# A second way to the v rows: tiles 1 to 5 gather u alone, and their v sums come from a product with the whole v table

## The chip, the cores and the metric

One core of one Trainium2 chip. The metric is the device time of the kernel in microseconds (us), the median of the runs. The engines are TensorE (PE), VectorE (DVE), ScalarE (ACT), GpSimd (POOL) and SyncE (SP, which issues most plain transfers).

## The reference, cut to what matters

A layer of a streaming encoder: a retention and short convolution block, then PEER, a retrieval of single-neuron experts per token, then a final norm. 1024 prompt tokens and 32 sample tokens, width 1024, all in float32. The part that the change touches:

```python
        s1 = jnp.einsum('thd,hnd->thn', q[:, :, 0], keys1)
        s2 = jnp.einsum('thd,hnd->thn', q[:, :, 1], keys2)
        v1, i1 = lax.top_k(s1, PEER_TOPK)
        v2, i2 = lax.top_k(s2, PEER_TOPK)
...
        eidx = jnp.take_along_axis(cidx, sel, axis=-1)
        gate = jax.nn.softmax(top_s.astype(jnp.float32), axis=-1).astype(xb.dtype)
        act = jax.nn.gelu(jnp.einsum('td,thkd->thk', xb, u_tab[eidx]))
        return jnp.einsum('thk,thkd->td', gate * act, v_tab[eidx])
```

Every token picks 8 heads x 16 = 128 of 16384 = 128 x 128 experts. With each it takes the dot product of its vector with a row of u, and adds a row of v, weighted by gate times gelu of the dot.

## The kernel before, in words

Tokens are worked in 8 tiles of 128 and a last tile of 32. A tile has 128 **steps**, one for each expert of a token: step g gathers one row of 8 KB for each of 128 tokens (u and v stand side by side in the table `uv`), 1.05 MB in one indirect DMA that POOL issues (L985). The rows land in a ring of 7 slots, 9 from step 616 on. Then, per step: DVE takes the dot product of the u half with the tile's vectors (L2050, a custom instruction and a read of its accumulator), ACT takes the gelu (L1225), multiplies by the gate (L1241) and scales the v half of the row by it (L1245), and PE adds the scaled half into PSUM by eight transposing products with the identity (L1625). The last of these frees the slot (`slot_free`), for which POOL waits before it gathers into it again. The last tile has 32 steps whose 128 rows belong to four experts of each of 32 tokens, summed by four products of 256 columns (L1571).

The rest of the layer is spread over these steps. Every engine runs one program in order; generators yield the step at which their next piece is put, and `advance` puts all that are due. So the projections (L1311, L1344), the retention of each tile, the product with w_out (L1406), the queries (L1508) and the scores of later tiles are computed on PE while earlier tiles are in their steps. DVE chooses the experts of one head of one tile at a time (`choices`: maxima and indices of 128 and 256 scores, L1852 to L1864, then L1965 to L1982), 71 such pieces in all; 41 of them stand in steps 128 to 767, 6 in steps 768 to 825 and 10 behind. L1786 adds a table to retention products, L1722 is one tap of the convolution. Weights come by SP through three buffers (`stream`).

At the end of a tile (`finish`) ACT copies the sum out of PSUM (L1193), PE turns it back (L1565), ACT and DVE norm it, and SP stores it.

```python
                for c in range(KC):
                    ins = pe.matmul(expert_sum[:, c * P:(c + 1) * P], row_of(g)[:, D + c * P:D + (c + 1) * P],
                                    ident_sb[:, :], is_transpose=True, start=False, stop=(g + 1 == end_of(t)),
                                    skip_group_check=True)
                ins.then_inc(slot_free, 1)
```

Of the kernel before, what the change touches and what calls it, by code (L numbers as in the profile page):

```python
# [59 lines left out]
QUADS_IN = 0  # L60
SPLIT = 2


RINGS = [(0, RING), (88 * RING, RING + 2)]


def slot_of(g):

    first, slots = [r for r in RINGS if r[0] <= g][-1]
    return (g - first) % slots  # L70
# [4 lines left out]

def lap_of(g):

    return SLOTS[:g].count(SLOTS[g])


def same_slot_before(g):

    return max((b for b in range(max(0, g - 2 * RING), g) if SLOTS[b] == SLOTS[g]), default=None)
# [71 lines left out]
def sums_before_x1(t):  # L155

    return t - 2


# [5 lines left out]
def sums_before_out(t):  # L165

    return sum(end_of(u) < out_at(t) for u in range(TILES + 1))
# [264 lines left out]
def layer_kernel(nc, xT, x, w_ret, w_conv, w_out, wq, keysT, uv, g_mix, g_ffn, g_fin, conv_par,  # L432
                 ret_state, cos_sin, decay_p, decay_s, edge_p, edge_s, block_decay, ident, sel, iota,
                 y, out_ret_p, out_ret_s, out_conv_p, out_conv_s):
    with ExitStack() as ctx:
# [33 lines left out]
        dots = sb("dots", [P, RINGS[-1][1]])  # L469
        weights = sb("weights", [P, RINGS[-1][1]])  # L470
# [40 lines left out]
        squares_last = last[:, 1792:1792 + QW]  # L511

# [99 lines left out]

        def first_out_bank(i):
            return [x1_ps[:, 0:D // 2], x1_ps[:, D // 2:3 * D // 4], mm[:, 1, 0:D // 4]][i]
# [68 lines left out]
        landed = [sem(f"landed{i}") for i in range(RINGS[-1][1])]  # L683
# [4 lines left out]
        y_out = [sem("y_out0"), sem("y_out1"), sem("y_out2")]  # L688
# [30 lines left out]
        def y_stored(eng, t):  # L719
            eng.wait_ge(y_out[t % 3], 16 * (t // 3 + (QUADS if t == SAMPLE else 1)))  # L720

        def store_quarter(eng, q):
            eng.dma_start(y[SEQ:TOK, q * QW:(q + 1) * QW],
                          y_last[q * DEC:(q + 1) * DEC, :]).then_inc(y_out[SAMPLE % 3], 16)
# [8 lines left out]
        def _(sp):  # L733
# [17 lines left out]
            def load_x_ahead(t):  # L751
                n, j = rows_of(t), group_of(t)
                yield mix_at(1) + 20 if t == 4 else first_use_at(j) - (26 if t < 5 else 64)
                if residual_stays(t):
                    if t == 2:
                        sp.wait_ge(projected, use_at(0, "ret", RING, 1) + 1)
                    wait(sp, sum_started, sums_before_x1(t))
                    if t == 3:
                        sp.wait_ge(projected, use_at(0, "B", 2, 1) + 1)
# [7 lines left out]
                if t == SAMPLE:  # L767
                    sp.wait_ge(sum_started, 3)
# [111 lines left out]
            def load_x(t):  # L880
# [7 lines left out]
                elif t in (4, 7):  # L888
                    yield end_of(t - 4) + 2
                    sp.wait_ge(sum_started, sums_before_x1(t))  # L890
# [24 lines left out]

            def store_y(t):
                n = rows_of(t)
                yield sum_root_at(t) + 5
                sp.wait_ge(y_ready, t + 1)
# [4 lines left out]
                sp.dma_start(y[t * P:t * P + n, :], xn[0:n, t % 2, :]).then_inc(y_out[t % 3], 16)  # L924

            def store_states():
# [13 lines left out]
                               *[load_cs(t) for t in range(TILES + 1)], *[store_y(t) for t in range(TILES + 1)], store_states())  # L940
# [4 lines left out]
            for t in range(TILES - 2, TILES + 1):  # L945
                y_stored(sp, t)


        @block.gpsimd
        def _(pool):  # L950
            for g in range(TOTAL):
# [10 lines left out]
                if same_slot_before(g) is not None:  # L962
                    pool.wait_ge(slot_free, same_slot_before(g) + 1)
                elif g >= RING:
                    pool.wait_ge(wout_done, SAMPLE + 3)
                else:
                    pool.wait_ge(projected, use_at(0, "ret", g, 1) + 1)
# [22 lines left out]
        def _(act):  # L990
# [21 lines left out]
            def projection(j):  # L1012
                for q, (kind, unit, t, slot) in enumerate(USES[j]):
# [17 lines left out]
                    if unit in (0, 4):  # L1031
                        wait(act, x1_ready, GROUPS[j][0])
                        if t == SAMPLE and unit:
                            act.wait_ge(sum_started, 4)
# [140 lines left out]
            def finish(t):  # L1175
                n = rows_of(t)
                yield end_of(t)
                if t == SAMPLE:
# [3 lines left out]
                    act.wait_ge(slot_free, end_of(t))  # L1182
# [5 lines left out]
                    act.wait_ge(y_ready, t + 1)  # L1188
# [3 lines left out]
                act.wait_ge(slot_free, end_of(t))  # L1192
# [3 lines left out]
                act.wait_ge(sum_back, t + 1)  # L1196
# [3 lines left out]
                act.wait_ge(sum_squared, 2 * t + 1)  # L1200
# [3 lines left out]
            programs = started(*[finish(t) for t in range(TILES + 1)],  # L1204
# [11 lines left out]
            for g in range(TOTAL):  # L1216
                t, k = tile_of(g)
                d = dots[:, SLOTS[g]:SLOTS[g] + 1]
# [7 lines left out]
                if t == SAMPLE:  # L1226
                    act.wait_ge(gelu_done, g + 1)
                    act.wait_ge(weighed, g + 1)
                    if k >= 3:
                        act.wait_ge(slot_free, g - 2)  # L1230
# [8 lines left out]
                act.wait_ge(gelu_done, g + 1)  # L1239
# [903 lines left out]
```

## Time and profile before

| what | value |
|---|---|
| runs of the kernel before, median | 2945.24 us (2944.16 to 2946.45, 3 runs) |
| span of the profiled execution | 2941.5 us |
| that execution's own time | the profile has none beside its span |
| busy: PE, DVE, ACT, POOL | 2311.9, 2077.7, 1968.4, 1258.5 us |
| moved | 1205.73 MB, mean 410 GB/s |
| gathers (queue q0) | 1107.36 MB, 91.2% of 16 engines' span |

Busy times are of instructions with their overlaps taken out; the mean of one instruction is longer than its share of the busy time where they are pipelined, as on PE. PEld is the loading of PE's stationary operand, which overlaps the products. PEclk is the granted clock of TensorE as a share of 2.4 GHz, the DMA share the busy share of the 16 DMA engines. An ordinary float32 product of PE stands in the trace as two records, a transposing one as one. The program's `x1_ps` is called `x_ps` in the profile.

### The profile page before, as it was taken

To read this page: it belongs to the slowest core of one execution; us is meant where nothing else is said; L and a number is where in the kernel's file an instruction comes from. 1 tells how busy PE (TensorE), PEld (TensorE's weight loads), DVE (VectorE), ACT (ScalarE), POOL (GpSimd) and SP (SyncE) were. 2 spreads that over 40 slices of the span, in tenths; PEclk is the share of its full clock that TensorE was granted. 3 is DMA by queue.
4 is the path that set the end of the run, shared out by engine and by line. 5 is a ranking of instruction groups with operands and counts; after the bars stand their busy time and mean duration, and the time that the engine had idled before them with its cause. 6 is when DMAs were issued, how large, how long until landed. Compare 5 with 4: busy or idle time off the path is not lost.

```text
span 2941.5 us, 36244 instructions
## 1 busy us (share of the span) xinstructions
PE 2311.9 (79%) x12548; PEld 1815.8 (62%) x12548; DVE 2077.7 (71%) x5143; ACT 1968.4 (67%) x3670; POOL 1258.5 (43%) x1063
## 2 busy tenths in 40 slices
PE   9988988987787777888987888778766666666777
PEld 8877777665565556665665555555655555555556
DVE  3677788675687887777666555788868787766444
ACT  2477666677676777666667676777767666767663
POOL 0233434444343444344444445334444445555653
PEclk9999999999987879999996988988767656666669
DMA  8899999999999999999999999999999999999998
GB/s 340 323 408 404 419 416 407 414 418 421 420 409 415 416 416 411 421 420 409 419 415 410 419 421 420 420 420 420 418 421 421 418 418 413 412 419 410 421 413 338
DMA packets 182055, 1205.73 MB, mean 410 GB/s; under 512 B 21744, under 2 KB 27184, under 8 KB 43504
## 3 DMA queue, kind: packets, MB, share of 16 engines
q0 software_dynamic: 152368, 1107.36, 91.2%
q1 hardware_dynamic: 29264, 95.93, 8.4%
q8 instruction: 99, 1.62, 0.2%
q14 instruction: 84, 0.69, 0.1%
q10 hardware_dynamic: 240, 0.13, 0.0%
HBM read 1198.48 MB, written 4.86 MB: 409 GB/s over the span
## 4 chain that ended last, share of the span: by engine, by line
DMA 42%; PE 22%; DVE 21%; ACT 10%; issue 4%; POOL 1%; SPq 0%; DVEq 0%; ACTq 0%; POOLq 0%
DMA ring<-in_uv,idx 38%; PE expert_sum L1625 9%; DVE ring L2050 9%; ACT ring L1245 4%; DMA w_out_sb<-in_uv,idx 4%; PE x_ps L1406 2%; PE mm L1508 2%; PE mm L1311 1%; ACT weights L1241 1%; PE x_ps L1344 1%; PE mm L1344 1%; DVE pairs_left L1855 1%; ACT L1225 1%; PE x_ps L1311 1%; PE expert_sum L1311 1%
## 5 line engine op out<-in xcount | busy, mean ns | idle before, releaser
L985 POOL DMA_INDIRECT ring<-in_uv,idx x958 | 1137.1, 1187 | 1534.0 <-PE expert_sum L1625 1328.1
L1625 PE MATMUL expert_sum<-ident_sb,ring 128*128 128x128 f32 x7472 | 1222.4, 319 | 516.6 <-ACT ring L1245 513.7
L2050 DVE CUSTOM_DVE_ANT_0 ring<-ring,xn 128x1024 f32<-128x1024 f32 x959 | 1168.1, 1222 | 616.9 <-DMA ring<-in_uv,idx 610.8
L1625 PEld LDWEIGHTS expert_sum<-ident_sb,ring 128*128 128x128 f32 x7472 | 1022.3, 165 | 782.5 <-ACT ring L1245 711.7
L1245 ACT ACTIVATE ring<-ring,weights 128x1024 f32<-128x1024 f32 x934 | 1073.0, 1149 | 30.4
L1225 ACT ACTIVATE dots<-dots 128x1 f32<-128x1 f32 x1056 | 211.4, 200 | 789.8 <-DVE dots L2050 786.9
L1241 ACT ACTIVATE weights<-dots,gate 128x1 f32<-128x1 f32 x1024 | 301.5, 294 | 38.3 <-DVE gate L1994 1.5
L1508 PE MATMUL mm<-xn_in,stream 128*128 128x416 f32 (+1 forms) x500 | 202.9, 531 | 0.0
L1625 PE MATMUL expert_sum<-ident_sb,w_out_sb 128*128 128x128 f32 x720 | 139.2, 358 | 70.0 <-ACT w_out_sb L1245 69.8
L1625 PEld LDWEIGHTS expert_sum<-ident_sb,w_out_sb 128*128 128x128 f32 x720 | 113.6, 186 | 98.7 <-ACT w_out_sb L1245 96.3
L985 POOL DMA_INDIRECT w_out_sb<-in_uv,idx x96 | 115.8, 1206 | 124.9 <-PE expert_sum L1625 110.4
L2050 DVE CUSTOM_DVE_ANT_0 w_out_sb<-w_out_sb,xn 128x1024 f32<-128x1024 f32 x97 | 118.5, 1223 | 68.3 <-DMA w_out_sb<-in_uv,idx 67.7
L1311 PE MATMUL mm<-stream,xn_in 128*128 128x256 f32 (+1 forms) x640 | 166.4, 395 | 0.0
L1311 PEld LDWEIGHTS mm<-stream,xn_in 128*128 128x128 f32 (+1 forms) x640 | 106.8, 182 | 22.4 <-issue 4.2
L1508 PEld LDWEIGHTS mm<-xn_in,stream 128*128 128x128 f32 x500 | 91.4, 204 | 40.9 <-issue 27.1
L1245 ACT ACTIVATE w_out_sb<-w_out_sb,weights 128x1024 f32<-128x1024 f32 x90 | 103.4, 1149 | 2.9
L2050 DVE DVE_READ_ACCUMULATOR2_ANT dots<- 128x1 f32 x1056 | 86.8, 82 | 0.0
L1344 PE MATMUL mm<-xn_in,stream 128*128 128x384 f32 (+1 forms) x232 | 84.3, 496 | 2.6 <-ACT conv_tmp L1028 2.3
L1225 ACT ACT_TABLE_LOAD x50 | 64.2, 1283 | 0.9
L1311 PE MATMUL x_ps<-stream,xn_in 128*128 128x256 f32 x256 | 64.0, 383 | 0.0
L1344 PE MATMUL x_ps<-xn_in,stream 128*128 128x128 f32 (+1 forms) x240 | 60.8, 400 | 0.0
L1571 PE MATMUL mm<-ring,stream 128*128 128x256 f32 x200 | 50.0, 399 | 9.3 <-ACT stream L1231 9.3
(405 smaller groups left out, 2218.3 us busy)
## 6 DMA issues: line engine op xcount, KB each, us to landing
stream<-in_wq SPq DMA_DIRECT2D x21, 1024.0 KB, 11.7
stream<-in_w_conv SPq DMA_DIRECT2D x16, 1024.0 KB, 11.3
stream<-in_w_ret SPq DMA_DIRECT2D x16, 1024.0 KB, 9.5
ring<-in_uv,idx POOLq DMA_INDIRECT x958, 13.9
ring<-in_w_ret SPq DMA_DIRECT2D x6, 1024.0 KB, 12.5
x<-in_x SPq DMA_DIRECT2D x8, 512.0 KB, 8.3
out_y<-xn SPq DMA_DIRECT2D x8, 512.0 KB, 8.2
stream<-in_w_out SPq DMA_DIRECT2D x3, 1024.0 KB, 9.7
```

The source lines that it names most:

```text
L985: pool.indirect_dma_start(row_of(g), None, uv, bass.IndirectOffsetOnAxis(ap=rows, axis=0)).then_inc(landed[SLOTS[g]], 16)
L1225: act.activation(d, d, ACT.Gelu_apprx_tanh).then_inc(gelu_done, 1)
L1241: act.activation(w, d, ACT.Copy, scale=gate[:, t % 5, k:k + 1]).then_inc(weighed, 1)
L1245: act.activation(v, v, ACT.Copy, scale=w).then_inc(scaled, 1)
L1311: ins = pe.matmul(bank[0:n, 0:UNIT], xnj[:, k, at:at + n], weight[k], start=(k == 0), stop=(k == KC - 1))
L1344: ins = pe.matmul(bank[:, 0:columns.stop - columns.start], weight[k], moving, start=(k == 0), stop=(k == KC - 1))
L1406: ins = pe.matmul(x1_ps[0:n, i * 512:(i + 1) * 512], lhsT, w_out_of(j, k)[:, i * 512:(i + 1) * 512], start=(k == 0), stop=(k == KC - 1))
L1508: ins = pe.matmul(query_bank(m, s), weight[s][k], xnT_of_pass(m)[:, k, :], start=(k == 0), stop=(k == KC - 1))
L1571: ins = pe.matmul(last_bank, of[0:rows, 96 - q * DEC:96 - q * DEC + P], values[0:rows, q * QW:(q + 1) * QW], start=begins and q == 0, stop ...
L1625: ins = pe.matmul(expert_sum[:, c * P:(c + 1) * P], row_of(g)[:, D + c * P:D + (c + 1) * P], ident_sb[:, :], is_transpose=True, start=Fals ...
L1855: ins = dve.match_replace(rest, values[:, 0:8], s, LOWEST)
L2050: dve.tensor_tensor_reduce(u, u, xn[:, t % 2, :], 1.0, 0.0, ALU.mult, ALU.add, dots[:, SLOTS[g]:SLOTS[g] + 1]).then_inc(dotted, 1)
```

## The change

Tiles 1 to 5 (`DENSE`) gather their u rows alone: half rows of 4 KB, into 8 halves of ring slots 0 to 3. Their 640 steps consist of the gather and the dot on DVE; no scaling on ACT and no expert sum on PE. The dots of a whole tile are kept (`tile_dots`).

`build(t)`, in the steps of the tile behind, makes the **spread weights** of tile t: ACT takes the gelu of all dots at once, DVE multiplies by the gates and splits each expert's number into its two halves of 7 bits, PE turns these. Then for each token one product of two one-hot matrices gives a 128 x 128 matrix that has the token's 128 weights at the places of its experts. One operand is made by DVE (`tensor_scalar` of 128x128, two scalars per partition, `hot_2`), the other by ACT (an Abs for each token and a Relu for four of them, `hot_1`). Four tokens form a group; a group is due every 3.75 steps, for tile 5 every 1.5. ACT copies a group out of PSUM into `staging` (16 KB per partition), and after every 8 groups SP stores 2 MB of it to DRAM (`w_spread`), 8.4 MB a tile. `staging` is there once: ACT waits for `w_stored` before the next copy.

`dense()` then multiplies. From step 826 (`DENSE_AT`) on, SP reads the v half of the table in 32 chunks of 512 rows (2 MB) and for each chunk and tile the spread weights (256 KB, six in flight). A **unit** is four products of 128x128 with 128x512 into one of two PSUM banks, half of a chunk's share of one tile; there are 32 x 5 x 2 = 320 units, three in two steps, up to step 1038. DVE adds every unit to the tile's sum in SBUF (128x512), which begins with the kept x1. Behind them `end_sums` norms the five tiles and SP stores them.

The ring has six slots from step 768 on (0 to 3 and the two in `w_out_sb`) and a seventh from step 826.

```diff
+DENSE = (1, 2, 3, 4, 5)
+FULL = [t for t in range(TILES + 1) if t not in DENSE]
+HALVES = 8
...
+def group4_at(t, q):
+
+    return build_at(t) + 3 + ((q * 15) // 4 if t != DENSE[-1] else (q * 3) // 2)
...
+def unit_at(n):
+
+    return DENSE_AT + (n * 2) // 3
...
+RINGS = [(0, tuple(range(RING))), (DENSE_END, (0, 1, 2, 3, RING, RING + 1)),
+         (BUILT + 2, (0, 1, 2, 3, RING, RING + 1, 4))]
...
+            def store_spread(t):
+
+                for b in range(BLOCKS):
+                    yield group4_at(t, (b + 1) * PER_BLOCK) + 2
+                    i = DENSE.index(t)
+                    sp.wait_ge(w_copied, i * GROUPS4 + (b + 1) * PER_BLOCK)
+                    sp.dma_start(w_spread[i, :, :, b * CHUNK * BLOCK:(b + 1) * CHUNK * BLOCK].rearrange("c p n -> p c n"),
+                                 staging.rearrange("p (c n) -> p c n", c=CHUNKS)).then_inc(w_stored, 16)
...
+                if is_dense(g):
+                    pool.indirect_dma_start(half_row_of(g), None, uv.rearrange("n (h d) -> (n h) d", h=2),
+                                            bass.IndirectOffsetOnAxis(ap=idx[:, t % 5, k:k + 1], axis=0)
+                                            ).then_inc(landed[LANDINGS[g]], 16)
+                    continue
```

ACT in `build(t)`:

```diff
+                for q in range(GROUPS4 + 1):
+                    yield group4_at(t, q)
+                    if q < GROUPS4:
+                        wait(act, w_built, r + q)
...
+                        for k in range(GROUP4):
+                            at = GROUP4 * q + k
+                            act.activation(hot_1[:, k, :], iota_sb2[:, :], ACT.Abs,
+                                           bias=turned_w[:, 0, at:at + 1]).then_inc(hot_1_steps, 1)
+                        act.wait_ge(hot_1_steps, (GROUP4 + 1) * (r + q) + GROUP4)
+                        act.activation(hot_1, hot_1, ACT.Relu, bias=one_sb[:, :],
+                                       scale=-1.0).then_inc(hot_1_steps, 1)
+                    if q:
+                        p = q - 1
+                        act.wait_ge(w_built, r + p + 1)
+                        if p % PER_BLOCK == 0:
+                            wait(act, w_stored, 16 * (i * BLOCKS + p // PER_BLOCK))
```

PE in `build(t)` and in `dense()`:

```diff
+                    for k in range(GROUP4):
+                        ins = pe.matmul(build_bank(t, q)[:, k * NK:(k + 1) * NK], hot_2[:, k, :],
+                                        hot_1[:, k, :], start=True, stop=True)
+                    ins.then_inc(w_built, 1)
...
+                    wait(pe, unit_added, n - 1)
+                    spread_w = w_rows[m % W_DEEP].rearrange("p (t i) -> p t i", i=CHUNK)
+                    for k in range(CHUNK):
+                        ins = pe.matmul(tp[:, n % 2, :], spread_w[:, :, k],
+                                        v_rows[c % V_DEEP][:, k, h * 512:(h + 1) * 512],
+                                        start=(k == 0), stop=(k == CHUNK - 1))
+                    ins.then_inc(unit_done, 1)
```

DVE in `build(t)` and in `dense()`:

```diff
+                    wait(dve, w_built, r + q)
+                    for k in range(GROUP4):
+                        at = GROUP4 * q + k
+                        dve.tensor_scalar(hot_2[:, k, :], iota_sb2[:, :], turned_w[:, 1, at:at + 1],
+                                          turned_w[:, 2, at:at + 1], ALU.is_equal, ALU.mult).then_inc(hot_2_ready, 1)
...
+                    half = sums[i][:, h * 512:(h + 1) * 512]
+                    dve.tensor_tensor(half, half, tp[:, n % 2, :], ALU.add).then_inc(unit_added, 1)
```

Where instructions come to stand, at two places. PE in tile 7 of the kernel before, eight transposes to a step and nothing else:

```order
L1565 MATMUL x1_ps<-ident_sb,xn 128x128 x8
L1625 MATMUL expert_sum<-ident_sb,ring 128x128 x40
L1625 MATMUL expert_sum<-ident_sb,w_out_sb 128x128 x16
L1625 MATMUL expert_sum<-ident_sb,ring 128x128 x56
L1625 MATMUL expert_sum<-ident_sb,w_out_sb 128x128 x16
```

PE of the change from step 822 on. L1909 is the expert sum, L1855 the product (`w_rows` lie in `xn_in` and `qkvg`, `v_rows` in `stream` and `ring`):

```order
L1909 MATMUL expert_sum<-ident_sb,ring 128x128 x32
L1855 MATMUL tp<-stream,xn_in 128x512 x8
L1909 MATMUL expert_sum<-ident_sb,ring 128x128 x8
L1855 MATMUL tp<-stream,xn_in 128x512 x4
L1909 MATMUL expert_sum<-ident_sb,ring 128x128 x8
L1855 MATMUL tp<-stream,xn_in 128x512 x8
L1909 MATMUL expert_sum<-ident_sb,ring 128x128 x8
L1855 MATMUL tp<-stream,xn_in 128x512 x4
```

Before every eight transposes of a step there now stand four or eight products of 512 columns.

ACT of the kernel before, in tile 6, where the sum of tile 5 has been copied out (L1193): one step after the other (L1225 the gelu, L1241 the gate, L1245 the scaling).

```order
L1193 ACTIVATE xn<-expert_sum 128x1024
L1225 ACTIVATE dots<-dots 128x1
L1241 ACTIVATE weights<-dots,gate 128x1
L1245 ACTIVATE ring<-ring,weights 128x1024
L1225 ACTIVATE dots<-dots 128x1
L1241 ACTIVATE weights<-dots,gate 128x1
L1245 ACTIVATE ring<-ring,weights 128x1024
```

ACT of the change in the steps of tile 6, where tile 5 is built (L1407 the Abs, L1410 the Relu, L1418 the copy into `staging`; L1457, L1473 and L1477 are the step's three):

```order
L1477 ACTIVATE ring<-ring,weights 128x1024
L1407 ACTIVATE ring<-ring 128x128 x4
L1410 ACTIVATE ring<-ring,one_sb 128x512
L1418 ACTIVATE ring<-x_ps 128x4x32x4
L1457 ACTIVATE dots<-dots 128x1
L1473 ACTIVATE weights<-dots,gate 128x1
L1477 ACTIVATE ring<-ring,weights 128x1024
L1407 ACTIVATE ring<-ring 128x128 x4
L1410 ACTIVATE ring<-ring,one_sb 128x512
L1418 ACTIVATE ring<-x_ps 128x4x32x4
```

Between the steps' scalings stand the six instructions of a group, the last of which also waits for a store at every eighth group.

## Rows read from the trace of the kernel before

**Rows 1.** Busy time of all engines in five stretches, core 0.
```profile
core 0: us, PE busy (x) PEld busy (x) DVE busy (x) ACT busy (x) POOL busy (x), PEclk, DMA share, GB/s
0.00:486.20 486.20, 434.51 (x2758) 382.29 (x2758) 339.69 (x963) 290.06 (x545) 149.52 (x139) 0.96 0.96 388
486.20:2208.80 1722.60, 1371.21 (x7436) 1022.32 (x7436) 1245.50 (x2997) 1206.05 (x2228) 744.45 (x643) 0.88 1.01 417
2208.80:2356.00 147.20, 97.32 (x480) 81.21 (x480) 119.68 (x329) 104.18 (x187) 62.61 (x57) 0.66 1.01 419
2356.00:2895.00 539.00, 374.10 (x1733) 304.55 (x1734) 351.60 (x822) 353.61 (x660) 289.94 (x213) 0.65 1.01 414
2895.00:2941.50 46.50, 34.74 (x143) 25.46 (x141) 21.26 (x36) 14.52 (x55) 11.96 (x12) 1.00 0.74 303
```

**Rows 2.** Waits from 486.2 to 2208.8 us: us in total, times, longest.
```profile
POOL ring L985 <- PE expert_sum L1625: 893.1, 530, 5.1
...
DVE ring L2050 <- DMA ring<-in_uv,idx: 397.2, 313, 3.7
...
DVE w_out_sb L2050 <- DMA w_out_sb<-in_uv,idx: 16.7, 13, 2.2
```

**Rows 3.** Timeline of ACT (start us, us): sums of tiles 0 and 5.
```profile
486.17 1.00 ACT L1193 ACTIVATE xn<-expert_sum 128x1024 f32<-128x1024 f32 x1
...
2208.79 1.01 ACT L1193 ACTIVATE xn<-expert_sum 128x1024 f32<-128x1024 f32 x1
```

**Rows 4.** The dot line alone on DVE, columns as in 1.
```profile
2208.80:2356.00 147.20, 70.15 (x116) 0.66 1.01 419
```

**Rows 5.** The expert sum line alone on PE, columns as in 1.
```profile
486.20:2208.80 1722.60, 786.76 (x5120) 661.57 (x5120) 0.88 1.01 417
```

**Rows 6.** DVE by line and shape: count, busy us, mean ns, idle before.
```profile
L2050 DVE CUSTOM_DVE_ANT_0 ring<-ring,xn 128x1024 f32<-128x1024 f32 x959 | 1168.1, 1222 | 616.9 <-DMA ring<-in_uv,idx 610.8
...
L2050 DVE DVE_READ_ACCUMULATOR2_ANT dots<- 128x1 f32 x1056 | 86.8, 82 | 0.0
...
L1967 DVE TENSOR_SCALAR half_i<-best_i 128x16 uint32<-128x16 uint32 x63 | 10.7, 169 | 0.0
...
L1786 DVE TENSOR_TENSOR turn<-tp,edge_p_sb 128x512 f32<-128x512 f32 x8 | 5.5, 688 | 7.9 <-PE tp L1379 7.9
...
L1722 DVE TENSOR_SCALAR conv_tmp<-conv_tmp,par 128x128 f32<-128x128 f32 x8 | 2.5, 310 | 0.9
```

**Rows 7.** ACT by line and shape, columns as in 6.
```profile
L1245 ACT ACTIVATE ring<-ring,weights 128x1024 f32<-128x1024 f32 x934 | 1073.0, 1149 | 30.4
...
L1241 ACT ACTIVATE weights<-dots,gate 128x1 f32<-128x1 f32 x1024 | 301.5, 294 | 38.3 <-DVE gate L1994 1.5
...
L1225 ACT ACTIVATE dots<-dots 128x1 f32<-128x1 f32 x1056 | 211.4, 200 | 789.8 <-DVE dots L2050 786.9
...
L1056 ACT ACTIVATE turn<-tp 128x512 f32<-128x512 f32 x16 | 8.6, 589 | 0.4 <-PE tp L1359 0.4
...
L1028 ACT ACTIVATE conv_tmp<-x_ps 128x128 f32<-128x128 f32 x4 | 1.0, 258 | 0.0
```

**Rows 8.** Timeline of PE: 512 column products and expert sums in turn.
```profile
1652.35 1.04 PE L1625 MATMUL expert_sum<-ident_sb,ring 128*128 128x128 f32 x8
1653.22 1.88 PE L1406 MATMUL x_ps<-w_out_sb,qkvg 128*128 128x512 f32 x4
1654.94 1.04 PE L1625 MATMUL expert_sum<-ident_sb,ring 128*128 128x128 f32 x8
```

**Rows 9.** PE by line and shape, columns as in 6.
```profile
L1406 PE MATMUL x_ps<-w_out_sb,qkvg 128*128 128x512 f32 x112 | 53.5, 600 | 0.0
...
L1344 PE MATMUL x_ps<-xn_in,stream 128*128 128x128 f32 x128 | 17.1, 292 | 0.0
```

**Rows 10.** Timeline of PE, one step of the last tile.
```profile
2928.81 1.99 PE L1571 MATMUL mm<-ring,stream 128*128 128x256 f32 x8 [0.49 <-ACT stream L1231]
```

**Rows 11.** DMA issues by line: KB each, us to landing.
```profile
w_out_sb<-in_w_out SPq DMA_DIRECT2D x1, 2048.0 KB, 23.7
```

More of the change, by code:

```diff
@@ L60, with build_at, is_dense, full_before @@
 QUADS_IN = 0
+QUADS_AT_V = 780
 SPLIT = 2
-RINGS = [(0, RING), (88 * RING, RING + 2)]
+DENSE = (1, 2, 3, 4, 5)
+FULL = [t for t in range(TILES + 1) if t not in DENSE]
+HALVES = 8
+DENSE_FIRST = DENSE[0] * STEPS
+DENSE_END = (DENSE[-1] + 1) * STEPS
+ROW_SLOTS = RING + 2
+GROUP4 = 4
+GROUPS4 = P // GROUP4
+BLOCK = 32
+BLOCKS = P // BLOCK
+PER_BLOCK = BLOCK // GROUP4
+CHUNK = 4
+CHUNKS = NK // CHUNK
+UNITS = CHUNKS * len(DENSE) * 2
+V_DEEP = 2
+W_DEEP = 6
+def build_at(t):
+    return (t + 1) * STEPS + 1
+def group4_at(t, q):
+    return build_at(t) + 3 + ((q * 15) // 4 if t != DENSE[-1] else (q * 3) // 2)
+BUILT = group4_at(DENSE[-1], GROUPS4) + 4
+DENSE_AT = BUILT + 2
+def unit_at(n):
+    return DENSE_AT + (n * 2) // 3
+def is_dense(g):
+    return DENSE_FIRST <= g < DENSE_END
+RINGS = [(0, tuple(range(RING))), (DENSE_END, (0, 1, 2, 3, RING, RING + 1)),
+         (BUILT + 2, (0, 1, 2, 3, RING, RING + 1, 4))]
 def slot_of(g):
     first, slots = [r for r in RINGS if r[0] <= g][-1]
-    return (g - first) % slots
+    return (g - first) % HALVES if is_dense(g) else slots[(g - first) % len(slots)]
 SLOTS = [slot_of(g) for g in range(TOTAL)]
-def lap_of(g):
-    return SLOTS[:g].count(SLOTS[g])
-def same_slot_before(g):
-    return max((b for b in range(max(0, g - 2 * RING), g) if SLOTS[b] == SLOTS[g]), default=None)
+def full_before(g):
+    return sum(not is_dense(b) for b in range(min(g, TOTAL)))
+def landing_of(g):
+    return SLOTS[g] // 2 + SLOTS[g] % 2 * (HALVES // 2) if is_dense(g) else SLOTS[g]
+LANDINGS = [landing_of(g) for g in range(TOTAL)]
+def lap_of(g):
+    return LANDINGS[:g].count(LANDINGS[g])
+def halves_of(g):
+    return (SLOTS[g],) if is_dense(g) else (2 * SLOTS[g], 2 * SLOTS[g] + 1)
+def steps_before(g):
+    near = {}
+    for b in range(max(0, g - 3 * STEPS * len(DENSE)), g):
+        for half in halves_of(b):
+            near[half] = b
+    found = {near[half] for half in halves_of(g) if half in near}
+    return (max((b for b in found if not is_dense(b)), default=None),
+            max((b for b in found if is_dense(b)), default=None))
+def full_index(t):
+    return sum(u < t for u in FULL)
 def rows_of(t):
@@ L152, in residual_stays @@
     return t < 4
-def sums_before_x1(t):
-    return t - 2
 def outs_before_back(t):
@@ L165, in sums_before_out @@
 def sums_before_out(t):
-    return sum(end_of(u) < out_at(t) for u in range(TILES + 1))
+    return sum(end_of(u) < out_at(t) for u in FULL)
 TURNS = [(x_turn_at(t), t, "x") for t in range(TILES + 1)]
@@ new lines, in end_sums @@
+            def end_sums():
+                yield unit_at(UNITS) + 2
+                act.wait_ge(unit_added, UNITS)
+                for i in range(len(DENSE)):
+                    act.activation(v_rows[i // CHUNK][:, i % CHUNK, :], sums[i], ACT.Square,
+                                   accum_out=end_stat[:, 0, i:i + 1]).then_inc(end_step, 1)
+                act.wait_ge(end_step, len(DENSE))
+                act.activation(end_stat[:, 0, :], end_stat[:, 0, :], ACT.Sqrt, bias=eps_sb[:, :],
+                               scale=1.0 / D).then_inc(end_step, 1)
@@ L1582, in _ @@
+            programs = started(warm_up(), rstd_row(), *[back(t) for t in FULL], *[build(t) for t in DENSE], dense(),
                                *[projection(j) for j in range(len(GROUPS))],
@@ new lines, in end_sums @@
+            def end_sums():
+                yield unit_at(UNITS) + 3
+                dve.wait_ge(end_step, len(DENSE) + 1)
+                dve.reciprocal(end_stat[:, 1, :], end_stat[:, 0, :]).then_inc(end_step, 1)
+                dve.wait_ge(end_step, len(DENSE) + 2)
+                for i in range(len(DENSE)):
+                    dve.scalar_tensor_tensor(sums[i], sums[i], end_stat[:, 1, i:i + 1], g_fin_sb[:, :],
+                                             ALU.mult, ALU.mult).then_inc(end_step, 1)
```

296 lines of the change are left out of this document (248 added, 48 removed).

## The prediction

> **What bounds the kernel now.** I read four views. First the busy time in stretches [rows 1]. The cuts are tile ends and step counts: the sum of tile 0 is copied out at 486.2 us and that of tile 5 at 2208.8 [rows 3], and the 116 dot instructions of the next 147.2 us are 58 steps [rows 4], so step 826 lies at 2356. In all three middle stretches the transfers are busy throughout (share 1.01, 414 to 419 GB/s) while no engine is. The transfers bound it: a step moves 1.05 MB and takes 1722.6 / 640 = 2.69 us. Second, who waits [rows 2]: POOL waits for the expert sum to free a slot, VectorE (DVE) for the gathered row, 413.9 us in the stretch of tiles 1 to 5. Nothing else holds a step. Third, the prices of single instructions [rows 6, 7, 9]. Fourth, TensorE (PE) where it is not kept waiting [rows 8]: that is where the new work goes. The granted clock is 0.65 to 0.66 from 2208.8 to 2895, where PE is 66 to 69% busy, almost only with transposes [rows 1].
>
> **The change, part by part.** By bytes it looks good: 640 half rows of 0.524 MB save 335.5 MB, or 804 us at 417 GB/s; the v table (67.1 MB) and the weights written and read (83.9 MB) cost 362 us. But bytes count only where the transfers still end last. So I go stage by stage.
>
> *Up to step 128*: nothing changes, 486.2 us [rows 1].
>
> *Steps 128 to 767.* Transfers: 1722.6 us at 0.417 MB/us are 718 MB; less 335.5, plus 36 of stored weights and kept x1, leaves 419 MB or about 1000 us. PE: 1371.2 us less the expert sums' 786.8 [rows 1, 5], plus 512 one-hot products (tiles 1 to 4; tile 5 is built later) of two records each, 2 x 17.1/128 = 0.27 us [rows 9], is 722. ACT: 1206.1 less 640 x (1.149 + 0.200 + 0.294) [rows 7] leaves 155; the builds add 32 groups a tile of 4 x 0.258 + 2 x 0.589 = 2.21 us (Abs, Relu, copy out [rows 7]), 283 for four tiles: 438. POOL stays at 744, its issues are as many as before. DVE keeps everything: the dot is still 1.222 + 0.082 = 1.304 us a step [rows 6], its choices and retention stay. 1245.5 us [rows 1], plus 512 one-hot operands. These are TENSOR_SCALAR of 128x128 with two scalars per partition; the nearest row is L1722's at 0.310, the lower bound L1967's at 0.169 [rows 6]. At 0.310 they are 159, small steps 5. Its idle time that is no wait for a gather stays, 1722.6 - 1245.5 - 413.9 = 63 [rows 1, 2]. Sum 1473; I take **1475**, 248 less than now. So DVE becomes the bound, and under 31% of the transfer saving is collected. Bounds: 1400 (one-hots at 0.169) and 1722.6 (as now, if waits between engines that the ring hides today all show).
>
> *Steps 768 to 825.* Full rows again, in 6 slots instead of 9, and tile 5's build in 48 steps. ACT has 104.2 us now [rows 1] and gets 70.7: 175, above today's 147.2. All weights leave by one staging buffer, in 4 stores of 2 MB; the copy after each store waits on ACT until it has landed, and behind it wait the scalings, so the expert sums, so the slots and the gathers. The nearest row is a 2 MB load beside gathers, 23.7 us to landing [rows 11]. Some 5 us pass before that copy, and the ring covers part of the rest: I charge 11 us each of four. **220**; bounds 147 (all hidden) and 270 (175 + 4 x 23.7).
>
> *Before the first unit*: the last store must land, then the first weights and v rows be read: **25**, between 5 and 48 (two landings). In tiles 1 to 4 the stores cost nothing since a group comes only every 3.75 steps (8.6 us) and DVE leaves ACT idle; without that cover it would be 16 times the same 11 us.
>
> *Steps 826 to 1038: the product.* 320 units; the order shows four products of 512 columns per unit, two for L1406's rows, which are four records in the trace. Four records take 1654.94 - 1653.22 = 1.72 us at full clock, eight expert transposes 1653.22 - 1652.35 = 0.87 [rows 8]. A unit is eight records, 3.44 us, and 320 are **1101**. Between them lie 198 expert sums of 0.87 (172) and 15 steps of the last tile of 1.99 [rows 10] (30). All on one engine, in order: **1303 us, where 539.0 stand now** [rows 1]. The mean over L1406's row, 53.5/112 = 0.478 a record [rows 9], gives 3.82 a unit and 1425: the upper end. Everything else hides under PE there: transfers 213 rows at 2.51 us (539.0/215) and 107 MB of v and weights at 415 GB/s are 792; DVE adds 320 x 0.688 = 220 [rows 6] to 352; ACT keeps 354. The two banks let a unit run while the one before is added, so DVE's adds cost PE nothing unless a piece of a choice between two adds exceeds a step of PE, 6 us.
>
> *The end*: 46.5 us as now [rows 1], plus 6.5 for five squares and scalings of 1024 columns (about 1 us each, as the copies in rows 3) ahead of the last steps' work: **53**, 46.5 to 60.
>
> Sum: 486.2 + 1475 + 220 + 25 + 1303 + 53 = 3562. The profile has no time beside its span of 2941.5; the median of the runs is 3.7 more, which I add: **3566 us**, 21% slower. All low ends together give 3391, all high ends 4015.
>
> A rule speaks on the unit. The row has 0.43 us for a record of 512 columns [rows 8], two streams of about 215 ns. The Trainium skill, page "TensorE: Matmul & The Clock Gate", section "Back-to-back issue gap", has 216 ns for an isolated matmul of 512 columns but about 131 ns in a sustained stream. The row stands by the former, though those are four records and no long stream; by the latter two streams would be 0.262, a unit 2.10, and the sum, by this estimate from the page, 3137.
>
> **The rivals.**
> *Tiles 1 to 5 gain nothing.* PE, ACT and DVE hand retention, scores and one-hots to each other; today a ring of rows covers each wait, and a DVE that is never idle covers none. For it: DVE works in order and would be 96% busy (1410 of 1475), so each late operand costs time at once. Against: only 63 us of its idle time now is no wait for a gather. Time 3566 + 248 = 3814.
> *The clock stays low in the product.* For: 0.65 in just these stretches now. Against: up to 486.2, with PE 89% busy, it is 0.96 [rows 1], and the product keeps PE busy without a break. At 1.2 GHz all of the 1303 doubles: 4869.
> *A long stream is cheaper.* Records of one shape without an expert sum in between may overlap more than the four of [rows 8]. The floor for one pass is the transposes' 0.87/8 = 0.109 per 128 columns, 0.435 for 512, or 1.74 a unit; half way between that and 3.44 is 2.59, and the total 3566 - 320 x 0.85 = 3294, still slower than now. Against: over all 112 records the mean is 0.478, not under 0.43 [rows 9]. The page named above goes further on this road.
> *Faster.* The products run in one pass, as the expert sums do: a unit 1.74, 320 x 1.74 + 202 = 759 us with the steps; then the transfers' 792 end last. With the low ends elsewhere 486 + 1400 + 147 + 5 + 792 + 46.5 + 3.7 = 2880. It decides below 2.04 us per unit with those low ends, below 1.50 with my own terms (1303 less the 621 that the change must make up is 682, less 202, over 320). Against: every ordinary f32 product of the trace has two records, only transposes one.
> *The change does nothing* would need the gathers to keep whole rows; the code addresses half rows, so I give it no more than the remainder.
>
> **How the numbers follow.** Forecast 0.76; no gain in tiles 1 to 5 0.10; low clock 0.04; cheaper stream 0.05; faster 0.02; slower by something unnamed 0.02; no difference 0.01. The likeliest case gives the time, 3566; its own range is 3430 to 3720, from ends that will not all fall on one side. The other cases stretch the top to 3800, which takes in part of the first rival; left out are the two lower cases (0.07), the low clock, half of the first rival, and the forecast's tails: 0.2. Low end 3420. Slower by over 0.2% (about what a measurement of this kernel can tell from no change) 0.97, within it 0.01, faster 0.02.
>
> **What would show it.** Right: DVE over 90% busy in tiles 1 to 5 with the DMA share well under 1 there, and tile 5's last dot near 1960 us; one-hot operands at 0.3 us; from about 2200 us PE full, granted clock 1.0, a unit every 3.44 us plus 0.87 per step, DMA share about 0.6; POOL waiting for the expert sum by far longest. Wrong: units spaced under 2.1 us, a clock of 0.5 to 0.7 there, the tail starting after 2450 (then the first part failed), or PE waiting in the tail for adds, v rows or weights, which would add to the 1303.

## The result, and the profile after

The changed kernel takes **3667.19 us** (median, 3661.81 to 3669.0 over 4 runs) against 2945.01: a ratio of 1.2446, 95% interval 1.2428 to 1.2463. The forecast was 3566, range 3420 to 3800, slower with 0.97. The first view of the profile after is the busy time in stretches, to be held against [rows 1], whose columns it has; the cuts are the first and last dot of tiles 1 to 5 (487.8 and 2006.4), the first product (2287.3) and the end of the last one (3613).

```profile
0.00:487.80 487.80, 435.80 (x2769) 383.89 (x2770) 337.28 (x960) 291.04 (x546) 143.20 (x136) 0.97 0.95 381
487.80:2006.40 1518.60, 898.20 (x3279) 594.89 (x3277) 1352.24 (x3520) 436.80 (x1031) 805.25 (x640) 0.75 0.79 272
2006.40:2287.30 280.90, 134.76 (x724) 119.10 (x724) 157.57 (x479) 178.53 (x381) 69.25 (x62) 0.67 0.81 298
2287.30:3613.00 1325.70, 1325.70 (x4288) 977.90 (x4289) 556.68 (x1137) 354.12 (x659) 271.36 (x212) 1.00 0.68 248
3613.00:3663.60 50.60, 37.65 (x148) 30.49 (x146) 26.61 (x41) 21.63 (x65) 16.71 (x14) 0.85 0.74 283
```

Three stretches, three bounds. In tiles 1 to 5 DVE is busy for 1352 of 1519 us, where the transfers bound before (share 1.01, now 0.79). In the product PE is busy for all of 1325.70 us, at a granted clock of 1.00, with the transfers at 0.68. Between them (2006.4 to 2287.3) no engine is, and the transfers are at 0.81: that is a stretch of waits. Waits of the whole span (us in total, times, longest):

```profile
POOL ring L1164 <- PE expert_sum L1909: 1039.0, 274, 35.2
POOL ring L1143 <- DVE ring L2401: 597.5, 291, 14.0
...
ACT ring L1418 <- DMA w_spread<-ring: 225.9, 17, 22.4
```

The gather waits for DVE's dot in tiles 1 to 5 (L1143) and for PE later (L1164). The old wait of DVE for the gathered row, 397.2 us in [rows 2], has shrunk to 32.6 there. L1418 is new: ACT waits for a store before a copy into `staging`, 225.9 us in all. PE in the product, its timeline as in [rows 8]:

```profile
2296.55 3.72 PE L1855 MATMUL tp<-stream,xn_in 128*128 128x512 f32 x8
2300.10 1.04 PE L1909 MATMUL expert_sum<-ident_sb,ring 128*128 128x128 f32 x8
2300.97 7.15 PE L1855 MATMUL tp<-stream,xn_in 128*128 128x512 f32 x16
2307.96 1.04 PE L1909 MATMUL expert_sum<-ident_sb,ring 128*128 128x128 f32 x8
```

A unit is eight records, as forecast, but it comes every 2300.10 - 2296.55 = 3.55 us when alone and in half of 6.99 when two stand together, not in 3.44.

Against the forecast, term by term:

| stretch | forecast us | measured us | how measured |
|---|---|---|---|
| to step 128 | 486.2 | 487.8 | first half-row dot |
| tiles 1 to 5 | 1475 | 1518.6 | to the last half-row dot |
| build of tile 5, to its last store | 220 | 240.7 | store issued at 2247.1 |
| to the first unit | 25 | 40.2 | 2287.3 |
| the product | 1303 | 1325.7 | to 3613 |
| the end | 53 | 50.6 | to the end of the span |
| outside the span | 3.7 | 3.6 | median 3667.2 less this span |

The last line of the table mixes two things: the profiled execution itself took 3665.39 us, 1.8 more than its span, and the median is another 1.8 above it. The terms were short by 101 us in all, and of the six that make up the span only the end was too high.

### The profile page after: what moved, and what is told of

The parts are those of the page before. It is cut to its first block, busy times and chain, and to the rows that moved or that the text cites. A ratio compares the mean times of both kernels' runs of the same rounds, so it can differ in the third digit from the quotient of the medians.

```text
span 3663.6 us, 34446 instructions
## 1 busy us (share of the span) xinstructions
PE 2832.1 (77%) x11203; PEld 2106.3 (57%) x11203; DVE 2430.4 (66%) x6133; ACT 1282.1 (35%) x2681; POOL 1305.8 (36%) x1063
## 4 chain that ended last, share of the span: by engine, by line
PE 46%; DVE 14%; DMA 10%; ACT 5%; issue 5%; SPq 0%; POOL 0%; ACTq 0%; DVEq 0%; POOLq 0%
PE tp L1855 31%; DMA w_spread<-ring 9%; DVE ring L2401 6%; PE expert_sum L1909 5%; PE expert_sum L1835 3%; PE mm L1740 2%; ACT ring L1407 2%; DVE ring L2337 2%; PE mm L1802 1%; ACT ring L1410 1%; PE x_ps L1576 1%; PE mm L1543 1%; PE x_ps L1638 1%; DMA xn_in<-w_spread 1%; DVE pairs_left L2141 1%
## 5 line engine op out<-in xcount | busy, mean ns | idle before, releaser
L1143 POOL DMA_INDIRECT ring<-in_uv,idx x640 | 803.9, 1256 | 726.9 <-DVE ring L2401 597.5
L1164 POOL DMA_INDIRECT ring<-in_uv,idx x332 | 392.8, 1183 | 1266.2 <-PE expert_sum L1909 1039.0
L2401 DVE CUSTOM_DVE_ANT_0 ring<-ring,xn 128x1024 f32<-128x1024 f32 x640 | 764.1, 1217 | 39.0 <-DMA ring<-in_uv,idx 32.6
L1835 PE MATMUL expert_sum<-ring 128*128 128x128 f32 x1024 | 214.4, 375 | 446.5 <-issue 326.5
L1457 ACT ACTIVATE dots<-dots 128x1 f32<-128x1 f32 x416 | 83.4, 200 | 1122.9 <-DVE dots L2407 1120.1
L2407 DVE CUSTOM_DVE_ANT_0 ring<-ring,xn 128x1024 f32<-128x1024 f32 x332 | 403.2, 1218 | 60.9 <-DMA ring<-in_uv,idx 58.5
L1909 PE MATMUL expert_sum<-ident_sb,ring 128*128 128x128 f32 x2480 | 349.3, 288 | 114.4 <-ACT ring L1477 113.7
L1909 PEld LDWEIGHTS expert_sum<-ident_sb,ring 128*128 128x128 f32 x2480 | 307.1, 149 | 194.4 <-ACT ring L1477 129.2
L1855 PE MATMUL tp<-stream,xn_in 128*128 128x512 f32 x864 | 390.9, 602 | 30.5 <-DMA xn_in<-w_spread 30.5
L1855 PE MATMUL tp<-ring,xn_in 128*128 128x512 f32 x864 | 390.1, 601 | 0.0
L1477 ACT ACTIVATE ring<-ring,weights 128x1024 f32<-128x1024 f32 x310 | 356.3, 1149 | 10.1
L1855 PEld LDWEIGHTS tp<-stream,xn_in 128*128 128x128 f32 x864 | 261.7, 310 | 120.4 <-issue 32.4
L1855 PEld LDWEIGHTS tp<-ring,xn_in 128*128 128x128 f32 x864 | 261.2, 310 | 87.2
L1407 ACT ACTIVATE ring<-ring 128x128 f32<-128x128 f32 x640 | 203.3, 390 | 202.1 <-PE expert_sum L1835 200.7
L2337 DVE TENSOR_SCALAR ring<-ring 128x128 f32<-128x128 f32 x640 | 188.6, 369 | 99.6 <-PE x_ps L1835 88.9
L1164 POOL DMA_INDIRECT w_out_sb<-in_uv,idx x82 | 103.7, 1264 | 349.7 <-PE expert_sum L1909 315.7
L1855 PE MATMUL tp<-stream,qkvg 128*128 128x512 f32 x416 | 190.2, 604 | 0.0
L1855 PE MATMUL tp<-ring,qkvg 128*128 128x512 f32 x416 | 189.6, 602 | 0.0
```

What stands on the lines that cost most here:

```text
L1143: pool.indirect_dma_start(half_row_of(g), None, uv.rearrange("n (h d) -> (n h) d", h=2), bass.IndirectOffsetOnAxis(ap=idx[:, t % 5, k:k + ...
L1164: pool.indirect_dma_start(row_of(g), None, uv, bass.IndirectOffsetOnAxis(ap=rows, axis=0)).then_inc(landed[SLOTS[g]], 16)
L1407: act.activation(hot_1[:, k, :], iota_sb2[:, :], ACT.Abs, bias=turned_w[:, 0, at:at + 1]).then_inc(hot_1_steps, 1)
L1477: act.activation(v, v, ACT.Copy, scale=w).then_inc(scaled, 1)
L1835: ins = pe.matmul(build_bank(t, q)[:, k * NK:(k + 1) * NK], hot_2[:, k, :], hot_1[:, k, :], start=True, stop=True)
L1855: ins = pe.matmul(tp[:, n % 2, :], spread_w[:, :, k], v_rows[c % V_DEEP][:, k, h * 512:(h + 1) * 512], start=(k == 0), stop=(k == CHUNK - 1))
```

## The experiments

The theory: the product costs what PE's float32 stream costs, whatever the transfers do; tiles 1 to 5 run at DVE's pace plus the stalls of the builds. The first four runs test both halves, the next four the sizes, the last two what was left. Each was measured once, but for the weights side by side (four times), so a small difference needs care. Four executions have exactly the same program up to the first product (the change, half the products, one pass, weights side by side), and it began at 2287.3, 2276.2, 2269.6 and 2273.8 us. With the build without the product a fifth shares tiles 1 to 5; these took 1509 to 1522 us. What a run gains ahead of the product is uncertain by up to 18 us, in tiles 1 to 5 by up to 12.

### Half the products

```diff
-                    for k in range(CHUNK):
+                    for k in range(CHUNK // 2):
                         ins = pe.matmul(tp[:, n % 2, :], spread_w[:, :, k],
```

> Each unit has two of its four products; the other half of the table's share is left out of the sums of tiles 1 to 5. Theory: TensorE's stream alone sets steps 826 to 1038, so they lose 320 x 1.72 = 550 us, from 1326 to 776, unless the transfers end last there: 330 MB at 417 GB/s are 792 us, at the 360 GB/s seen in that stretch 917. So 780 to 920 us for the stretch and a time of 3120 to 3260. Rival: the stretch is set by something that does not shrink with the products (weights or v rows arriving, DVE's additions), and the time stays within 50 us of 3667. Everything before step 826 as in the changed kernel: 2287 us.

Measured: 3150.28 us. The stretch of the product:

```profile
2276.20:3098.00 821.80, 792.29 (x3007) 586.39 (x3008) 549.91 (x1137) 353.87 (x659) 270.43 (x212) 0.98 1.00 398
```

It fell by 504 us, from 1326 to 822, and its DMA share went from 0.68 to 1.00: PE's stream had set the stretch. With half of it the transfers are busy throughout, but PE too is for 792 us, so this run alone does not say which of the two ends last. The 360 GB/s of the expectation was no limit of these transfers; 398 flow as soon as they are wanted.

### Products in one pass

`short_w` shows the weights as pairs of 16 bits, of which the product takes the upper one.

```diff
-                    spread_w = w_rows[m % W_DEEP].rearrange("p (t i) -> p t i", i=CHUNK)
+                    short_w = w_rows[m % W_DEEP].bitcast(mybir.dt.bfloat16).rearrange("p (t i s) -> p t i s", i=CHUNK, s=2)
...
-                        ins = pe.matmul(tp[:, n % 2, :], spread_w[:, :, k],
-                                        v_rows[c % V_DEEP][:, k, h * 512:(h + 1) * 512],
+                        ins = pe.matmul(tp[:, n % 2, :], short_w[:, :, k, 1],
+                                        v_rows[c % V_DEEP][:, k, h * 512:(h + 1) * 512].bitcast(mybir.dt.bfloat16)[:, 1::2],
```

> The products take the upper 16 bits of both operands as bf16, so the v sums of tiles 1 to 5 lose precision; the same transfers, additions and steps. Theory: a float32 product is two records of two passes each, a bf16 product one record of one pass, so a product falls from 0.86 to 0.22 us, a unit from 3.5 to 0.9, and TensorE needs 320 x 0.9 + 205 = 493 us for a stretch that transfers then set: 790 to 920 us, the same as with half the products or below it by little. Time 3120 to 3260. Rival (the price is in the loading of strided weights or in the issue, not in the passes): a unit stays over 2 us.

Measured: 3122.22 us, the stretch 802 us (2269.6 to 3071.5) at a DMA share of 1.01 and 407 GB/s. The timeline:

```profile
2498.34 1.08 PE L1855 MATMUL tp<-ring,qkvg 128*128 128x512 bf16 x4
2499.26 1.03 PE L1909 MATMUL expert_sum<-ident_sb,ring 128*128 128x128 f32 x8
```

A unit is four records and 2499.26 - 2498.34 = 0.92 us, where float32 has eight and 3.5. The additions, the transfers and the strided reads of the weights are as before, so the price lay in how PE works through float32 operands. Here PE is busy for only 566 of the 802 us: the transfers end last, for which the prediction had worked out 792 us.

### The half rows without any v sum

`build`, `dense`, `store_spread`, `load_v` and `load_spread` are taken out of the lists of programs, and the waits on them with them.

```diff
-            programs = started(*[finish(t) for t in FULL], *[build(t) for t in DENSE], dense(), end_sums(),
+            programs = started(*[finish(t) for t in FULL],  end_sums(),
```

> No spread weights are built, stored or multiplied: the v sums of tiles 1 to 5 are left out, their gathers of u rows and their dots stay. It shows the most that the half rows can give. Theory: DVE sets tiles 1 to 5, 1245.5 us of work as in the kernel before and some 63 us of waits, 1310 in all, and the rest runs as before (733 us from step 768 on): 488 + 1310 + 733 + some 15 for the norms, 2530 to 2580 us. Rival: eight half rows in flight and their latency, or the 4 KB pieces, set the stage, at 1400 us or more and with DVE waiting over 150 us for gathers.

Measured: 2532.81 us, tiles 1 to 5 in 1299:

```profile
490.00:1788.60 1298.60, 672.98 (x2244) 405.07 (x2242) 1217.96 (x2980) 115.54 (x244) 802.88 (x640) 0.74 0.85 295
```

DVE is busy for 94% of it and the transfers for 85%; DVE waited 29.5 us for half rows. So 412 us is the most that half rows in five tiles can give here, and DVE sets it. The rival of latency is out.

A 4 KB half row also costs the transfers more than half of a row. From 500 us on, the gathers of this run (331.30 MB up to 1780 us) took 74.9% of the 16 engines' time; before the change 580.55 MB up to 2000 us took 93.5%. That is 346 against 414 GB/s of busy engines: half the bytes for 60% of the time. With DVE out of the way the transfers would hold the stretch at about 0.85 x 1299 = 1104 us (an estimate from this run's row).

### Stores in long pieces

```diff
-                    sp.dma_start(w_spread[i, :, :, b * CHUNK * BLOCK:(b + 1) * CHUNK * BLOCK].rearrange("c p n -> p c n"),
-                                 staging.rearrange("p (c n) -> p c n", c=CHUNKS)).then_inc(w_stored, 16)
+                    sp.dma_start(w_spread[i, :, b, :], staging).then_inc(w_stored, 16)
```

> The spread weights lie in DRAM by partition, so that a store of 2 MB goes in pieces of 16 KB instead of 512 B, and the reads behind step 826 in pieces of 512 B instead of 2 KB. Theory: the stores took 18 to 38 us because of their 4096 pieces of 512 B, ACT waited 226 us for them, and through it the builds and all that shares ACT and TensorE. With long pieces ACT's wait for the stores falls under 60 us, tiles 1 to 5 take 1420 to 1480 us instead of 1519, steps 768 to the first unit 220 to 250 instead of 281: 3540 to 3600 in all. Rival 1: the waits were beside the path, DVE's own work sets the stage, and the time stays within 20 us of 3667. Rival 2: the short reads now stall the units, and the last stretch grows beyond 1340 us.

Measured: 3601.84 us, 65 less than the change. Waits of this run: ACT's for stores in the whole span, and DVE's for the scores from 488 to 1960 us, which was 45.4 us in the change:

```profile
ACT ring L1419 <- DMA w_spread<-ring: 86.4, 13, 15.6
...
DVE top_v L2139 <- ACT scores L1334: 6.6, 4, 3.6
```

226 became 86, not under 60. Tiles 1 to 5 took 1471 us (488.8 to 1960), inside the expectation; the last dot to the first unit took 262 instead of 281, above it. The product took 1328 us instead of 1326, so the short reads cost next to nothing beside PE. The waits for the stores were on the path in part: 140 us less of them gave 65 us, or 47 if the fastest of the four starts of the product above is taken for the base.

How a store holds up DVE can be read in the trace of the change, three of its instructions in order of time (start us, us):

```profile
869.33 0.60 ACT L1418 ACTIVATE ring<-expert_sum 128x512 f32<-128x512 f32 x1 [13.47 <-DMA w_spread<-ring]
869.82 0.38 ACT L1333 ACTIVATE scores<-tp 128x256 f32<-128x256 f32 x1
...
870.23 0.30 DVE L2138 MAX8 top_v<-scores 128x8 f32<-128x128 f32 x1 [9.18 <-ACT scores L1333]
```

ACT's copy waits 13.47 us for a store, the copy of the scores stands behind it on ACT, and DVE waits 9.18 us for these scores. With long stores DVE's wait for scores is all but gone.

### Weights side by side

```diff
-                        ins = pe.matmul(tp[:, n % 2, :], spread_w[:, :, k],
+                        ins = pe.matmul(tp[:, n % 2, :], w_rows[m % W_DEEP][:, k * P:(k + 1) * P],
```

> The product takes its 128 stationary columns side by side instead of every fourth one, so weights and tokens are mixed up and the sums of tiles 1 to 5 are not the reference's; number, size and timing of everything else stay. Loading the spaced columns takes 308 ns in the changed kernel's trace, 190 for L1406's columns in the kernel before, and single units come every 3.55 us instead of 3.44. Theory: that difference is the loading, which shows once per unit where the record before it is short; 320 units lose 0.05 to 0.11 us each, 16 to 35 us, and the time is 3632 to 3651. Rival: loading hides under the records in any case, and the time stays within 6 us of 3667.

Measured: 3638.38 us (median of four, 3628.75 to 3643.97; ratio to before 1.2356, interval 1.2335 to 1.2377, below that of the change). The loads of the stationary operand, first in the changed kernel, then here (min/median/max in ns):

```profile
L1855 PEld LDWEIGHTS tp<-stream,xn_in x864: 307/308/337, 2287.3 to 3557.4; 128*128 128x128 f32 x173
```

```profile
L1855 PEld LDWEIGHTS tp<-stream,xn_in x864: 190/190/338, 2273.7 to 3521.9; 128*128 128x128 f32 x173
```

and its timeline in the product:

```profile
2501.43 3.60 PE L1855 MATMUL tp<-ring,qkvg 128*128 128x512 f32 x8
2504.87 1.04 PE L1909 MATMUL expert_sum<-ident_sb,ring 128*128 128x128 f32 x8
```

Units come every 2504.87 - 2501.43 = 3.44 us, and the product takes 1304 us (2273.8 to 3577.8), the 1303 of the prediction. The missing 22 us of that term were the spaced columns. The medians differ by 29 us; the other 7 are not the product's. The profiled execution, the fastest of the four, reached the product 13.5 us before the change did, with the same program up to there.

### One of four one-hot operands

```diff
-                    for k in range(GROUP4):
+                    for k in range(1):
                         at = GROUP4 * q + k
                         dve.tensor_scalar(hot_2[:, k, :], iota_sb2[:, :], turned_w[:, 1, at:at + 1],
```

> DVE makes one of the four one-hot operands of a group and TensorE uses it four times, so three tokens in four get wrong spread weights. 480 instructions of 0.295 us of DVE's busy time go, 384 of them (113 us) in tiles 1 to 5. Theory: DVE's work sets those tiles, so they take 1519 - 113 = 1406 us, and the time is 3530 to 3570. Rival: other waits in the builds (for the store, for ACT's half) take their place, the tiles lose less than 50 us and the time is over 3610.

Measured: 3600.11 us; tiles 1 to 5 in 1458 us (488.4 to 1946.2), 61 less, between theory and rival. DVE's busy time there fell by 98, to 1254.5, but its waits grew: for scores 52.6 us (45.4 in the change), and for PE before the operand 33.5 (9.5):

```profile
DVE top_v L2138 <- ACT scores L1333: 52.6, 6, 17.2
DVE ring L2337 <- PE expert_sum L1835: 33.5, 9, 13.0
```

(The waits are those from 488 to 1945 us.) So DVE's work sets only part of the stage; behind it stands the chain of the builds, in which ACT waits for stores (251.4 us in this run).

### The build without the product

The same lists without `dense`, `load_v` and `load_spread`; `build` and `store_spread` stay.

```diff
-                               *[store_spread(t) for t in DENSE], load_sums(), load_v(), load_spread(),
+                               *[store_spread(t) for t in DENSE], load_sums(),
```

> The spread weights are built and stored as in the change, but never read and never multiplied: the v sums of tiles 1 to 5 are left out. It prices the parts before the product. Theory: tiles 1 to 5 and the build of tile 5 as in the changed kernel (487.8 + 1518.7 + 240 us up to about step 824), and from step 826 on the time of the kernel before, 539.0 + 46.5, and 12 for the norms of the five tiles: 2840 to 2870 in all, some 800 us less than the change. Rival: the steps behind 826 run slower than before even without the product, because the ring has seven slots there instead of nine: then more than 2900.

Measured: 2867.6 us, as expected. The stretch from step 826 on, up to the end:

```profile
2251.00:2865.80 614.80, 418.22 (x1922) 339.40 (x1922) 388.78 (x890) 385.89 (x747) 303.73 (x234) 0.68 1.00 409
```

The granted clock is 0.68 there, where the change has 1.00 in its product and the kernel before 0.65. PE is busy for 68% of the stretch, almost only with transposes. With the end it takes 614.8 us, 17 more than the 539.0 + 46.5 + 12 of the expectation; whether that is the smaller ring was not tried.

### Long stores and one pass

Both edits together.

> Long stores and one-pass products together: float32 products taken in bf16, spread weights stored in pieces of 16 KB. It is the fastest form of the change that the runs so far point to. Theory: the two savings lie in different stretches and add up: 3122 - 65 = 3057, between 3040 and 3075. Rival: the 512 B reads, harmless beside a slow product, now slow a stretch that the transfers set, by 10% of their 42 MB or more, so that the time stays over 3085.

Measured: 3109.67 us, not 3057. The first product came at 2223.4, where the long stores alone had 2222.6 and the one-pass run 2269.6, so 46 us were gained ahead of it. But the product took 834 us instead of 802, at 392 GB/s instead of 407 with the engines as busy (DMA share 1.03 and 1.01). The rival holds: reads in pieces of 512 B, free beside a slow product, cost 32 us in a stretch that the transfers set.

### Long stores and one one-hot operand

> Long stores and one of four one-hot operands on DVE together; three tokens in four get wrong spread weights. Alone, long stores took 48 us off tiles 1 to 5 (1518 to 1471) and the operands 61 of the 113 us that their removal frees on DVE. Theory: each was held up by the other's wait in the same chain of groups, so that together they free more than the sum, 113 to 150 us: tiles 1 to 5 in 1370 to 1405 us. Rival: the two parts are independent and add up, 109 us: 1409 or more. Floor: 1298, what the tiles took without any build.

Measured: 3521.17 us; tiles 1 to 5 in 1391 us (492.3 to 1883.1). Together the two free 128 us of 1519; alone 47 and 61. That is 20 us more than the sum, and between 17 and 29 whichever of the five executions with the same program is the base. So each was in part held up by the other, as the theory had it, by a margin not far above the uncertainty of single runs. Above the floor of 1299 are left 92 us for the rest of the build.

### Long stores, weights ahead of the sums

```diff
-                               *[store_spread(t) for t in DENSE], load_sums(), load_v(), load_spread(),
+                               *[store_spread(t) for t in DENSE], load_spread(), load_sums(), load_v(),
```

> Long stores as before, and SP issues the first six loads of spread weights ahead of the kept sums (2 MB) and the second chunk of v rows (2 MB) instead of behind them. Theory: the first unit waits 29 us because its 256 KB stand behind 4 MB on the same queues; ahead of them they land within 10 us, the first unit starts 15 to 22 us sooner and the time is 3580 to 3588 instead of 3602. Rival: the wait is the gathers', which fill the same engines, and the time stays over 3596.

Measured: 3592.88 us, 9 less than with long stores alone, where 14 to 22 were expected and the rival began at less than 6. Nine us of a single run decide nothing by themselves; the trace does. PE's wait for the first weights was 29.3 us there and is 15.6 here:

```profile
2209.88 10.16 PE L1856 MATMUL tp<-stream,xn_in 128*128 128x512 f32 x16 [15.64 <-DMA xn_in<-w_spread]
...
2224.55 3.79 PE L1856 MATMUL tp<-stream,xn_in 128*128 128x512 f32 x8 [3.64 <-DVE keys_sb L2353]
```

(L1855 of the change is L1856 in this file.) Half of the wait was the 4 MB ahead; what the other half is was not tried. Part of the gain is given back: the third unit waits 3.64 us for DVE's addition, which now waits for the sums.

## Why the prediction was right, point by point

The forecast was 101 us low, within its range, and its main mechanism is shown: DVE bounds tiles 1 to 5, PE the product. The misses are in sizes and in one wait.

**The unit** was right to the record. What failed, by 22.7 us, is the price in "a unit is eight records, 3.44 us": it came from L1406, whose columns lie side by side, and the change reads every fourth one. With them side by side the product took 1304 us. The rivals on it are settled: the stream is not cheaper when it is long (3.44 a unit with neighbouring columns, over 320 units), and the clock is 1.00. The last rival, that the change is faster, needed a unit below 2.04 us; in the run with one pass it was 0.92, and the kernel was still slower, 3122 us.

The rule of the Trainium skill, page "TensorE: Matmul & The Clock Gate", section "Back-to-back issue gap", that a sustained stream of 512 columns spaces at 131 ns instead of 216, does not hold here. The float32 records space at 0.43 us, which is twice the page's 216 and not twice its 131, and four bf16 records take 0.92 us, 0.23 each.

**"Everything else hides under PE there"** held: the DMA share was 0.68, and the 792 us put on the transfers came out as 802 and 822 when the product was made short.

**Tiles 1 to 5** came 43.6 us over the 1475. The base, 1245.5 + 63 = 1308, came out as 1299 without builds, in part by luck: DVE was busy for 1218 us, 27 less, and idle for 81, 18 more. The builds then add 220 us to it instead of the 164 of the sum (159 and 5). Their work on DVE is smaller than forecast, 134 us (1352 less 1218): an operand takes 0.341 us in the median, but 384 of them taken out freed only 98 us of busy time, 0.254 each. The step that failed is "its idle time that is no wait for a gather stays, 63": DVE idles for 166 us, of which 33 are waits for half rows, so 134 are not.

Much of that idle time goes back to "in tiles 1 to 4 the stores cost nothing", which was wrong. ACT waited 179 us for them before the last half-row dot (13 times, up to 22.4 us), DVE waited behind ACT for scores, and long stores alone took 47 us off the stage. The cover named there, 8.6 us between two groups, is shorter than a store: on the critical chain the stores of tiles 1 to 4 took 18 to 38 us. The first rival, that hand-overs between the engines show once DVE has no slack, was thus right in part: 204 of the forecast's 248 us were gained. DVE was busy for 89% of the stretch, not over 90.

Off the bound the same stretch was sized worse, without effect: PE was busy for 898 us instead of 722, POOL for 805 instead of 744, and the transfers for 0.79 x 1519 = 1200 us instead of about 1000. Most of that is there without the builds (1104 us, 0.85 x 1299), since half rows take more than half the time of whole ones.

**Steps 768 to 825** took 240.7 instead of 220. Up to the last store ACT was busy for 167.4 us against the 175 of the sum, and waited 46.9 for stores against the 44. The term put at nothing is the dots: ACT waited 27.6 us for them, and DVE, which makes them, waited 88.9 us for PE's one-hot products there. With the dots the three fill the stretch.

**Before the first unit** 40.2 instead of 25: the store landed after 11.0 (2247.1 to 2258.1), the weights after 29 more. 4 MB of sums and v rows were asked for ahead of them, and putting the weights first took 14 off PE's wait.

**The fate of the byte saving** is what matters. From single runs: half rows alone give 412 us (2945 to 2533); building and storing the weights takes 335 (2533 to 2868); the product 800 (2868 to 3667), of which 255 are left if a unit costs PE 0.92 us instead of 3.5 (3122). No version beats the kernel before: the fastest form tried is at 3110, and even with no product at all only 77 us are gained.

## What to carry to other kernels

Bytes saved are worth time only up to the point where the next engine ends last: here DVE took the bound after half of the saving (412 of the 804 us that the bytes are worth), and the work that replaced the bytes went to an engine that had no room for it. Count a dense product on PE in records times the price per record before counting what it saves, and look up how the stationary columns lie. A single buffer with a store behind it needs the store's time between two uses, even where its engine is idle by more than half, and whatever stands behind the wait on that engine is late for others.

## What the runs showed of the hardware

- Loading 128 stationary float32 columns took 308 ns with every fourth one taken and 190 with neighbours; it showed as 0.05 to 0.11 us per unit of eight records, 22 us over 320 units (runs of the change and of the weights side by side).
- A bf16 product of 512 columns is one record, and four of them came in 0.92 us; the float32 one is two records, and four products took 3.44. The granted clock was 1.00 where these were read.
- Gathered half rows of 4 KB took 60% of the transfer time of rows of 8 KB, for half the bytes.
- Stores of 2 MB in pieces of 512 B and in pieces of 16 KB: ACT's waits for them went from 226 to 86 us. Reads of 42 MB in pieces of 512 B instead of 2 KB cost 32 us where the transfers were the bound.
